# Other orders at a one-core encoder layer's first rows, gates and first branch panel, and V12 and V22 loaded by quarters in turn

## The reference

```python
def mixing_block(u, ...):
    proj = u @ w_in                     # 1024 x 5120: h, b, c, q, k, v (512 each), gates (2 x 1024)
    inner = cc * hc
    conv = inner[s-1]*conv_w[0] + inner[s]*conv_w[1] + inner[s+1]*conv_w[2]
    y_conv = (bc * conv) @ w_conv_out
    # 4 heads; per head two maps, with a linear distance bias
    a = softmax(s1) - lam * softmax(s2) # lam from lambda_qk
    o = rmsnorm(a @ v, subln_g) * (1 - lam_init)
    y_attn = o @ w_attn_out
    g = sigmoid(gates + b_gate)         # 1024 x 2 x 1024
    return (g[:, 0] * y_conv + g[:, 1] * y_attn) @ w_o

u = rmsnorm(x, norm_g[0]); h = x + rmsnorm(mixing_block(u, ...), norm_g[1])
u = rmsnorm(h, norm_g[2]); f = square(relu(u @ w_ff1)) @ w_ff2      # 1024 -> 4096 -> 1024
out = h + rmsnorm(f, norm_g[3])
```

## Time and profile before

| | |
|---|---|
| median of 3 runs | 1398.29 us (1398.01 to 1399.68) |
| the profiled execution | 1399.42 us, of which the span is 1397.70 |
| granted TensorE clock, mean | 0.997 |
| busy in the span | PE 98%, PE weight loads 80%, DVE 71%, ACT 43%, GpSimd 8% |
| moved by DMA | 162.02 MB, 116 GB/s in the mean |

### The profile page before, as it was taken

How to read it: one execution, slowest core, us unless ns; L and a number is a source line. 1 busy time by engine, 2 the same in 40 slices (tenths; PEclk the granted TensorE clock), 3 DMA queues, 4 the chain that set the end, 5 groups by cost and what they waited for, 6 DMA issues and landing times.

```text
span 1397.7 us, 17147 instructions
## 1 busy us (share of the span) xinstructions
PE 1370.8 (98%) x6209; PEld 1116.8 (80%) x6209; DVE 989.5 (71%) x1425; ACT 600.6 (43%) x929; POOL 112.5 (8%) x73
## 2 busy tenths in 40 slices
PE   7999999999999999899999999999999999999998
PEld 6778777777778788688888888888888778888886
DVE  7787796886989754466566787676665597765676
ACT  6544544544544444501243453333332354444454
POOL 0000000000000000000000323333323100000000
PEclk9999999999999999999999999999999999999999
DMA  5111111101111332354732155444445964336343
GB/s 185 46 31 31 30 31 30 45 15 38 37 30 54 109 117 90 110 157 150 253 105 75 53 179 189 137 155 155 144 158 188 382 215 148 98 108 209 106 129 112
DMA packets 141613, 162.02 MB, mean 116 GB/s; under 512 B 6829, under 2 KB 88938, under 8 KB 141418
## 3 DMA queue, kind: packets, MB, share of 16 engines
q1 hardware_dynamic: 135392, 148.14, 33.2%
q10 hardware_dynamic: 6154, 13.01, 2.4%
HBM read 114.98 MB, written 46.14 MB: 115 GB/s over the span
## 4 chain that ended last, share of the span: by engine, by line
PE 85%; DVE 6%; DMA 4%; ACT 2%; issue 2%; ACTq 0%; SPq 0%; DVEq 0%
PE psum L866 34%; PE psum L983 23%; PE psum L1136 19%; PE psum L904 2%; PE psum L1113 2%; PE psum L949 2%; DMA f_raw<-f_scratch 2%; PE psum L953 1%; DVE g_sum L1862 1%; DMA gates_scratch<-staging 1%; DMA w_raw<-in_w_in 1%; ACT staging L1291 1%; PE psum L1085 1%; DVE w_lo L1686 0%; DVE dev L1828 0%
## 5 line engine op out<-in xcount | busy, mean ns | idle before, releaser
L1136 PE MATMUL psum<-op 128*128 128x512 f32 x1344 | 305.6, 389 | 2.1 <-DVE op L2170 2.0
L1136 PEld LDWEIGHTS psum<-op 128*128 128x128 f32 x1344 | 252.1, 188 | 55.5 <-issue 3.3
L866 PE MATMUL psum<-act_hi,w_hi 128*128 128x512 f32 x448 | 182.0, 406 | 1.1 <-DVE act_lo L1680 1.1
L866 PE MATMUL psum<-act_hi,w_lo 128*128 128x512 f32 x448 | 175.2, 391 | 0.0
L866 PE MATMUL psum<-act_lo,w_hi 128*128 128x512 f32 x448 | 174.6, 390 | 0.0
L2167 DVE TENSOR_TENSOR op<-v,op 128x512 fp32r<-128x512 f32 x112 | 78.5, 700 | 85.0 <-ACT op L1541 84.8
L1541 ACT ACTIVATE op<-v 128x512 fp32r<-128x512 f32 x112 | 70.6, 631 | 139.1 <-PE psum L1136 125.1
L866 PEld LDWEIGHTS psum<-act_hi,w_hi 128*128 128x128 f32 x448 | 84.2, 188 | 21.3 <-issue 3.4
L866 PEld LDWEIGHTS psum<-act_lo,w_hi 128*128 128x128 f32 x448 | 84.3, 188 | 18.0 <-issue 1.9
L866 PEld LDWEIGHTS psum<-act_hi,w_lo 128*128 128x128 f32 x448 | 84.1, 188 | 18.2
L2170 DVE TENSOR_TENSOR op<-f_raw,op 128x512 fp32r<-128x512 f32 x112 | 77.8, 695 | 17.4 <-ACT op L1543 17.4
(11 more groups left out here) (265 smaller groups left out, 2802.6 us busy)
## 6 DMA issues: line engine op xcount, KB each, us to landing
f_raw<-f_scratch SPq DMA_DIRECT2D x112, 256.0 KB, 2.7
w_raw<-in_w_in SPq DMA_DIRECT2D x34, 512.0 KB, 4.7
w_raw<-in_w_ff SPq DMA_DIRECT2D x32, 512.0 KB, 5.0
f_scratch<-f_out SPq DMA_DIRECT2D x56, 256.0 KB, 2.4
gates_scratch<-staging ACTq DMA_DIRECT2D x32, 256.0 KB, 2.0
gate_in<-gates_scratch SPq DMA_DIRECT2D x16, 512.0 KB, 4.3
v<-in_w_ff SPq DMA_DIRECT2D x8, 1024.0 KB, 8.5
v<-in_w_ff SPq DMA_DIRECT2D x4, 2048.0 KB, 12.1
```

What stands on the lines that cost most here:

```text
L866: mm = nc.tensor.matmul(bank, stat(a, kt), moving(b, kt), start=(n == 0), stop=(n == len(terms) - 1))
L1136: mm = nc.tensor.matmul(psum[:, (X_BANK, Z_BANK)[m % 2][t]], op[n % SLOTS][:, 2 + a, token_cols(t)], op[n % SLOTS][:, b], start=(m in (0, ...
```

## The change

Six edits:

1. *First rows.* The sum of squares of row tile 3 moves from DVE to ACT. The load of `lambda_qk` moves from ACT's queue to SP's, behind row tiles 4 to 7.
2. *Gates' first pair.* ACT copies X1 before it splits T4, and X2 before the tanh of C11.
3. *Gates' later pairs.* C21's sum has a second buffer: `prod[3]` in every other pair. ACT copies X2 before the tanh of the pair before's C21.
4. *First branch panel.* ACT and DVE split its weights and OS2, OS3 before the last pair's C22, C11, C12 and C21. PE waits for `o_lo` only at the first product that reads it.
5. *V12 and V22.* Both come in quarters of 1 MB, V12 behind F blocks 6, 10, 14, 18 and V22 behind 8, 12, 16, 20.
6. *MLP's third panel.* DVE makes its `lo` part before the first half of T2's sum.

```diff
+SUM_ROWS = ((0, 2, 3, 4, 6), (1, 5, 7))
...
-        v11_landed = [sem(f"v11_landed{n}") for n in range(4)]
+        v1_landed = [sem(f"v11_and_v22_landed{n}") for n in range(4)]
         v12_landed = [sem(f"v12_landed{n}") for n in range(4)]
-        v21_landed, v22_landed = sem("v21_landed"), sem("v22_landed")
+        v21_landed = sem("v21_landed")
...
+        def gate_kept(k, p):
+            return prod[3] if k == 1 and GATE.slot(p) else GATE.sums[k]
...
                 if h == 0:
                     head_panels(0, range(2))
+            sp.dma_start(lqk[:].rearrange("p n c -> p (n c)"),
+                         lambda_qk.rearrange("l n c -> l (n c)").to_broadcast([P, 4 * HD])).then_inc(lqk_landed, 16)
             head_panels(0, range(2, HEAD_PANELS))
...
                 f_load(n)
-                if n in (6, 7, 8, 9):
-                    v_load(v12, 0, 1, 4 * (n - 6), 4, v12_landed[n - 6])
-                elif n in (10, 12):
-                    v_load(v22, 1, 1, (n - 10) // 2 * (STEPS // 2), STEPS // 2, v22_landed)
+                if n in (6, 10, 14, 18):
+                    v_load(v12, 0, 1, n - 6, 4, v12_landed[(n - 6) // 4])
+                elif n in (8, 12, 16, 20):
+                    v_load(v22, 1, 1, n - 8, 4, v1_landed[(n - 8) // 4])
...
             pe.wait_ge(zlo_ready, CT)
-            pe.wait_ge(olo_ready, HEADS)
...
                             src = (z_hl, o_hl)[br]
+                            if (j, h, br) == (0, 0, 1):
+                                pe.wait_ge(olo_ready, HEADS)
...
-            act.dma_start(lqk[:].rearrange("p n c -> p (n c)"),
-                          lambda_qk.rearrange("l n c -> l (n c)").to_broadcast([P, 4 * HD])).then_inc(lqk_landed, 16)
...
             row_sum(2)
             row_deviation(2)
+            row_sum(3)
             row_deviation(3)
             split_hi(0, 0, 0)
...
+                elif k == 2:
+                    if p > st.first + 1:
+                        act.wait_ge(gate_ready, GATE_AT[2 * p - 3, 0])
                 elif p > st.first:
-                    act.wait_ge(gate_ready, GATE_AT[((2 * p - 2, 0), (2 * p - 1, 0), (2 * p - 1, 1))[k - 1]])
-                nc.scalar.activation(st.sums[k - 1][:], psum[:, st.slot(p)], ACT.Copy
+                    act.wait_ge(gate_ready, GATE_AT[((2 * p - 2, 0), None, (2 * p - 1, 1))[k - 1]])
+                dst = gate_kept(k - 1, p) if st is GATE else st.sums[k - 1]
+                nc.scalar.activation(dst[:], psum[:, st.slot(p)], ACT.Copy
...
             last_turn("g6")
-            t_hi_part(GATE, 4)
             for p in range(GATE.first, GATE.end - 1):
...
                 x_copy(GATE, 1, p)
+                if p == GATE.first:
+                    t_hi_part(GATE, 4)
                 g_part_hi("W11", p + 1)
                 if p > GATE.first:
                     gate_block("C12", p - 1)
                 g_part_hi("S4", p)
+                if p == GATE.first:
+                    x_copy(GATE, 2, p)
                 gate_block("C11", p)
                 if p > GATE.first:
+                    x_copy(GATE, 2, p)
                     gate_block("C21", p - 1)
-                x_copy(GATE, 2, p)
...
             g_part_hi("S4", p)
+            x_copy(GATE, 2, p)
             gate_block("C21", p - 1)
-            x_copy(GATE, 2, p)
...
             x_copy(GATE, 3, p)
+            act.wait_ge(mix_done, GATE.at("Y", p))
+            split_hi(P_BR, P_BR % RING, P_BR // RING)
+            last_turn("OS2 OS3")
             gate_block("C22", p)
-            last_turn("OS2")
             gate_block("C11", p)
-            split_hi(P_BR, P_BR % RING, P_BR // RING)
-            last_turn("OS3")
             gate_block("C12", p)
             gate_block("C21", p)
...
             scale_rows(2)
-            row_sum(3)
             scale_rows(3)
...
             last_turn("OS0 OS1")
+            split_lo(P_BR, P_BR % RING)
+            last_turn("OS2 OS3")
             gate_sum("C22", p)
-            last_turn("OS2")
             gate_sum("C11", p)
-            split_lo(P_BR, P_BR % RING)
-            last_turn("OS3")
             gate_sum("C21", p)
...
-                    dve.wait_ge(v22_landed, 32)
+                    dve.wait_ge(v1_landed[kt // 4], 32)
...
             t_lo(FF1, 3)
+            w1_lo(2)
             t_sum(FF1, 2, 0)
-            w1_lo(2)
             t_sum(FF1, 2, 1)
```

More of the change, by code:

```diff
@@ L1181, in row_sum @@
                 act.wait_ge(x_landed[t], 16)
-                wait(act, row_sums[0], t // 2)
+                wait(act, row_sums[0], SUM_ROWS[0].index(t))
                 nc.scalar.activation(xsq[0][:], xn[:, t], ACT.Square, accum_out=stats[:, t:t + 1]
@@ L1304, in gate_block @@
                     act.wait_ge((f11_sum, f21_sum, f22_sum)[k], GATE.n(p) + 1)
-                    gate(panel, h, GATE.sums[k][:])
+                    gate(panel, h, gate_kept(k, p)[:])
             def g_part_hi(x, p):
@@ L1693, in row_sum @@
                 dve.wait_ge(x_landed[t], 16)
-                wait(dve, row_sums[1], t // 2)
+                wait(dve, row_sums[1], SUM_ROWS[1].index(t))
                 vec.tensor_tensor_reduce(out=xsq[1][:], in0=xn[:, t], in1=xn[:, t], scale=1.0, scalar=0.0,
@@ L1903, in gate_sum @@
                 dve.wait_ge(mix_done, GATE.at(("Y", "Z2", "Z1")[k], p))
[L1904 removed]
+                kept = gate_kept(k, p)
+                vec.tensor_tensor(kept[:], psum[:, (2, 4, 4)[k] + GATE.slot(p)], kept[:], ALU.add
                                   ).then_inc((f11_sum, f21_sum, f22_sum)[k], 1)
```

10 lines of the change are left out of this document (5 added, 5 removed).

## The result

The changed kernel took 1391.78 us (median of 6 runs, 1391.29 to 1392.59), the kernel before 1398.28 (6 runs, 1398.01 to 1399.68): 0.995 of the time, 95% interval 0.9939 to 0.9961, that is 5.5 to 8.5 us less. Forecast were 1391.3 within 1388.0 to 1395.5. The profiled execution took 1391.34, beside the 1399.42 of before, so 8.08 us are to be found between the two traces; the sum of the terms was 8.1. By the medians the gain is 6.5 us.

A forecast was written before the change was run, and what follows sets the result against it. PE was taken to bound the kernel, busy 1370.8 of 1397.7 us. Terms 0.26 + 0.25 + 0.46 + 4.10 + 0.68 + 2.35 = 8.1 off 1399.42 gave 1391.3 us, range 1388.0 to 1395.5.

The forecast's parts named there:

- new gap before the first pair's X4: First gates' pair: X4 waits 3.3 us for ACT's copy of X3; old gaps go, net gain 0.25 us.
- gap before the last Z2: Last gates' pair: PE idles 2.8 us until DVE's C22 sum; the branch then starts 1.70 us earlier.
- second pair's X3: Second gates' pair: the wait of 0.30 for X2's copy goes with `prod3` as second buffer, gain 0.46 us.
- clock: Branch start: after 2.8 us idle before Z2 the clock stays at 2.4 GHz, so 2.40 us are gained.
- matmuls of 0.63 behind a new gap: Sign of being wrong: matmuls lasting 0.63 us after the gap before the first pair's X4 or the last Z2.
- first rows: Kernel start: `w_hi` at best 0.67 us earlier, first product gains 0.26 us, bounds 0 and 0.67.
- V quarters: Last stage, loads of V12 and V22: both PE gaps go with no new wait, gain 2.35 us.
- second branch panel's `w_lo`: Branch loop: ends near 591.7 while PE needs it at 597.9, a cover of 6 us, so no cost.
- nothing new is late: Rival: C22's sum and X3's first copy do not hold PE, gain 15.3 us, 1384.1 us; chance 0.08.
- V rival: Last stage: V loads still hold F blocks, gaps of 2.35 us stay or move, 1393.7 us; chance 0.12.
- slower one: Rival at the V loads: every quarter holds an F block, eight PE gaps of 1.18 us, 1400.7 us; chance 0.03.
- the clock falls: Rival: half clock behind gaps before first X4 and last Z2, 2.40 us each; chance 0.15 for one, 0.06 both.

The follow-up runs named there:

- a_x3: Changed kernel with the first pair's X3 copy ahead of S2's and S3's copies on ACT, and the second pair's X2 copy ahead of C11's tanh: 1389.88 us.
- a_c22: Changed kernel with C22's sum on DVE moved ahead of the first branch panel's `w_lo` and the last two `o_lo`: 1390.24 us, ratio 0.9944.
- b_pair1: Kernel before with only the first gates' pair's order changed (X1's copy ahead of `g_t4_hi`, X2's ahead of C11's tanh): 1399.93 us, ratio 1.0004.
- b_rows: Kernel before with only the first rows' part: row tile 3's sum on ACT, `lambda_qk` issued later on SP: 1398.73 us, ratio 0.9994.
- b_sum: Kernel before with only row tile 3's sum moved to ACT, `lambda_qk` left on ACT's queue: 1398.94 us, ratio 1.0.
- b_vq: Kernel before with only the loads of V12 and V22 in quarters: 1396.41 us, ratio 0.9977.
- a_all: Changed kernel with X3's copy ahead of S2's and S3's in every pair but the last, C22's sum early and the tail's tanh moved later: 1382.40 us, ratio 0.9878.

## Why the prediction was right, and where it wasn't

**Right in place and in size.** The new gap before the first pair's X4, on ACT's copy of X3 behind S2's copy (3.3 forecast, 3.38 found); the gap before the last Z2 on C22's sum behind nine low parts (2.8 and 2.73), with a branch start of 586.95 forecast on the old axis and 586.08 + 0.86 = 586.9 found; the full clock there in all three traces of the changed kernel. Read from durations of before, the queue on DVE predicted the new wait within a tenth. a_x3 and a_c22 show these causes: the gap goes when that copy or that sum moves (a_x3 also moves a copy of the second pair, which comes after the gap). The second pair's X3 was right in size (0.46 and 0.59), but its cause isn't shown, as b_pair1 has the gain without the edit.

**Wrong: the clock behind the first pair.** The step "clock" of the branch was read over to 3.3 us of idle time, and the forecast left a fall there to a rival, at 0.15 for one and 0.06 for two. In all five traces with the gap of 3.4 the clock fell. This was one of the prediction's own signs of being wrong, matmuls of 0.63 behind a new gap. But the price that the rival put on it, 2.40, was too high: 1.46 to 1.7. The branch's 2.40 came from a half clock of 6.8 us, of which PE worked 4.9; behind the new gap it lasted 3.4. The term is -1.21, not +0.25. At the branch, the full clock behind 2.8 us was taken by nearness to one row with 2.29; it came true in the changed kernel and not in a_x3, so that term was partly luck.

**Wrong: the first rows.** The step said "at best `w_hi` starts 0.67 earlier". It took the landing of the weights as fixed up to its own wait. It moved by 2.0, mostly since `lambda_qk`'s load ran ahead of both the rows and the weights (b_rows against b_sum). With `w_hi` and `w_lo` out of the way the start is set by the transposes, and so by when the clock rises, which the sum left out. The 0.26 itself, counted from the first `act_hi`, is near what the order buys where the clock rises as late as in the trace of before. The other 1.0 of the 1.24 is a clock that rose 1.9 us earlier in the profiled run, which is luck. Over all nine profiles with the new start the first product is at 14.31 to 15.25, median 14.68, over the four with the old one at 15.00 to 15.55, median 15.36: 0.7 rather than 0.26 or 1.24.

**Nearly right: the V quarters**, 2.35 forecast and 2.57 found, in all three traces of the change (2.58 in b_vq). **Also late:** the second branch panel's `w_lo`, forecast near 591.7 on the old axis and found near 594.8, as the tanh waited for their stores; the cover of 6 us was 3. It cost nothing until a_c22. **Missing:** the wait on `f_out`, 0.66, of which 0.34 stay.

So against the forecast +0.98 at the start, +0.24 in the heads, +0.22 at the V loads, +0.17 in the MLP, +0.13 at X3 and +0.04 at the branch made up for -1.46 in the first pair and -0.34 at `f_out`. The number was hit by terms that cancel; the range held it on better grounds. Of the rivals, "nothing new is late" was wrong as the change stands, at 1384.1; a_all, which takes each new lateness away, is there with 1382.4. That is close in time, but a_all has another order than the change, with the tail's tanh moved too. The V rival and the slower one fell with b_vq. The rival "the clock falls" was right in one of its two gaps.

## What to carry to other kernels

When a wait before an in-order engine goes, read on in the same queue for what its next reader needs: here each copy moved ahead only exposed the next one, until C22's sum, X3's copies and the tail's tanh had moved too, and then the gain more than doubled. An instruction that another engine waits for belongs ahead of work that itself waits for a third engine, even if it was never late so far: the second pair's copy was covered by a gap one pair earlier. And price a new gap on TensorE twice, for its length and for the half clock behind it; trading two gaps of 2.3 and 1.0 us for one of 3.4 lost 1.2 to 1.5 us in the traces, of which 0.6 came back one pair later. A stretch that is late is also forgiven where the next wait doesn't move with it: look there before you count a loss as it stands.
